# RWKV projections: the next tile's raw keys are loaded a step sooner, the key row goes to another buffer and ahead of the bonus product, and the table loads and removals are reordered

## The chip, the cores and the metric

One core of one Trainium2 chip. The metric is the device time of the whole program in microseconds. The kernel before was run three times: median 3709.45 us, from 3708.74 to 3713.39.

## The reference, cut to what is computed

The program is two blocks of layers over 1024 tokens of width 1024, in fp32. The change is in the RWKV layer of the second block, in the stage that makes its six streams. The part that matters:

```python
xx = token_shift(hn) - hn
xs = hn[None] + xx[None] * mu[:, None, None, :]
r, k, v, g = jnp.einsum('pbsd,pdf->pbsf', xs[:4], w_in)
w_log = -jax.nn.softplus(-(w0 + jnp.tanh(xw @ w1) @ w2)) - 0.5
decay = jnp.exp(-jnp.exp(w_log.astype(jnp.float32)))
a = jax.nn.sigmoid(a0 + (xa @ a1) @ a2)
kk = (k * k_k).reshape(B, S, H, N).astype(jnp.float32)
kk = kk / jnp.maximum(jnp.linalg.norm(kk, axis=-1, keepdims=True), 1e-12)
k = k * (1.0 + (a - 1.0) * k_a)
# the scan over time uses r, decay, k, v, kk, a; then
bonus = jnp.sum(rh * kh * r_k, axis=-1, keepdims=True) * vh
```

## The kernel before

`rwkv_projections` (L3879) runs from about 2559 to 3081 us of the span. Its main loop has sixteen steps j: four streams (k, r, v, g) of four steps, each step two tiles of 128 tokens. A step is a product of two tiles by a 1024x1024 weight, done in seven sums of eight matmuls instead of eight (`Seven`, L950): TensorE's order in a step is sum 5, sum 6, sum 3, sum 7, then sum 1 of the next step, sum 4, and sum 2 of the next step. GpSimd (POOL below) makes the operand sums s1, s2, s4, s3 for the step after; it runs about a step ahead. VectorE takes results out of PSUM (p15, u2, then the removals c12, c22, c21; L1040 to L1060) and ends each step with `mix(j + 2)`: a subtraction (L4137) and eight multiply-adds (L4140). ScalarE (ACT below) copies p1 and removes c11. Each engine works in the order in which its instructions are written; the semaphores only hold it up.

Beside steps 5, 6, 8, 9, 10, 12, 13 and 14 (`STEP_OF`, L3646) runs one tile of `ScanRows` (L3640), which turns the raw rows of the streams, read back from DRAM, into the rows that the scan of the next stage reads: cumulated decays, normed keys, the x, r, b and k rows, and the bonus. Its buffers are eight 128x1024 rows: `row_r`, `row_k`, `row_a`, `row_w`, `kk`, `t1`, `upto`, `back`. For one tile:

- SP loads `row_k`, `row_a`, `row_w`, `row_r` (L3697 to L3708), each once the rows in that buffer have been used or stored; the load of `row_a` waits until the b row of the tile before has landed in DRAM (L3707).
- POOL makes the keys `kk` (L3811); ACT squares them into `back` (L3782), makes `t1` = a - 1 (L3787), and the exponential `upto` of the decay sums (L3791) that TensorE makes from `row_w` (L3774). ACT then takes Ln of the head sums (L3793), the reciprocal decays into `back` (L3795), the norm (L3797), scales sixteen heads (L3801) and takes the exponential of `row_w` (L3803).
- VectorE reduces the squares (L3843, L3845), adds to the decay sums (L3850), and makes the key in `row_k` (L3861), the r row (L3868), the b scaling (L3855), the bonus rows (L3874) and their sums (L3876). In its order, the key and the r row stand between c12 and c22, the b scaling and the bonus between c22 and c21.
- POOL makes less (`t1` times k_a, L3816), the bonus product (L3821), the x row (L3827), the b row (L3832) and the k row (L3838); SP stores them.

In a POOL step the order is: keys, s1, less, s2, s4, bonus product, s3, x row, b row, k row. On SP the order in a step with a tile is: c11 store, ends, c12 store, c22 store, x row store with the next `row_w` load, c21 store, r row store with the next `row_r` load, b row store, k row store with the next loads of `row_k` and `row_a`. The activation tables are loaded by the compiler in front of each function that the present table lacks; `one_table` (L125) asks for a table that holds both Ln and Exp.

Of the kernel before, what the change touches and what calls it, by code (L numbers as in the profile page):

```python
# [10 lines left out]
ACT = mybir.ActivationFunctionType  # L11
# [3628 lines left out]
class ScanRows:  # L3640
# [95 lines left out]
    def sp_b_row(self, sp, i):  # L3736
        sp.wait_ge(self.q["b_row_made"], i + 1)
        sp.dma_start(self.raw[5][self.at(i), :], self.row_a).then_inc(self.q["b_stored"], 16)

    def sp_k_row(self, sp, i):  # L3740
        sp.wait_ge(self.q["k_row_made"], i + 1)
        sp.dma_start(self.raw[1][self.at(i), :], self.back).then_inc(self.q["k_stored"], 16)
        if i + 1 < X_TILES:
            self.sp_load_k(sp, i + 1)
            self.sp_load_a(sp, i + 1)

    def sp_rows(self, sp):
        first = self.at(0)
# [28 lines left out]
    def act_rows(self, act, i):  # L3777
        q = self.q
        act.wait_ge(q["kk_made"], i + 1)
        if i:  # L3780
            act.wait_ge(q["k_stored"], i * 16)
        act.activation(self.back, self.kk, ACT.Square).then_inc(q["squared"], 1)  # L3782
        act.wait_ge(q["ones_made"], 1)
        act.wait_ge(q["a_in"], (i + 1) * 16)
        if i:
            act.wait_ge(q["key_made"], i)
        act.activation(self.t1, self.row_a, ACT.Identity, bias=self.minus_one[:, :]).then_inc(q["less_made"], 1)  # L3787
        act.wait_ge(q["L_made"], i + 1)
        if i:
            act.wait_ge(q["r_stored"], i * 16)  # L3790
        act.activation(self.upto, self.sum_banks, ACT.Exp).then_inc(q["upto_decayed"], 1)  # L3791
        act.wait_ge(q["sums_floored"], i + 1)
        act.activation(self.norm[:, :], self.norm[:, :], ACT.Ln).then_inc(q["ln_made"], 1)  # L3793
        act.wait_ge(q["before_summed"], i + 1)
        act.activation(self.back, self.sum_banks, ACT.Exp, scale=-1.0).then_inc(q["back_decayed"], 1)  # L3795
        act.wait_ge(q["ln_made"], i + 1)
        act.activation(self.norm[:, :], self.norm[:, :], ACT.Exp, scale=-0.5).then_inc(q["rnorm_made"], 1)  # L3797
        act.wait_ge(q["rnorm_made"], i + 1)
        for h in range(W_HEADS):
            one = self.kk[:, h * W_DIM:(h + 1) * W_DIM]  # L3800
            last = act.activation(one, one, ACT.Copy, scale=self.norm[:, h:h + 1])  # L3801
        last.then_inc(q["kk_normed"], 1)
        act.activation(self.row_w, self.row_w, ACT.Exp).then_inc(q["own_decayed"], 1)  # L3803
# [30 lines left out]
    def pool_k_row(self, pool, i):  # L3834
        q = self.q
        pool.wait_ge(q["key_made"], i + 1)
        pool.wait_ge(q["b_row_made"], i + 1)
        pool.tensor_tensor(self.back, self.row_k, self.back, ALU.mult).then_inc(q["k_row_made"], 1)  # L3838

    def dve_sums(self, dve, i):  # L3840
        q = self.q
# [37 lines left out]
def rwkv_projections(nc, core, a, raw, weights, room, scan, row_sums):  # L3879
# [8 lines left out]
    with ExitStack() as mem:  # L3888
# [44 lines left out]
        with nc.Block() as block:  # L3933

            @block.sync
            def _(sp):
                sp.dma_start(norm_columns[:, :], columns_of(a["norm_gain_2"][1]), allow_slow_non_contiguous=True).then_inc(small_in, 16)
                for n in range(6):
                    sp.dma_start(mu[:, n, :], columns_of(a["odd_mu_2"][0, n]), allow_slow_non_contiguous=True).then_inc(mu_in, 16)
                for m, (down, up, bias) in enumerate((("rwkv_w1_2", "rwkv_w2_2", "rwkv_w0_2"), ("rwkv_a1_2", "rwkv_a2_2", "rwkv_a0_2"))):  # L3940
                    sp.dma_start(w_down[:, m, :, :], weight_blocks(a[down][0])).then_inc(lora_in, 16)
                    sp.dma_start(w_up[0:LO, m, :], a[up][0]).then_inc(lora_in, 16)
                    sp.dma_start(w_up[LO:LO + 1, m, :], a[bias][0].unsqueeze(0)).then_inc(lora_in, 16)
                scan.sp_constants(sp)

                def store(j, made, count, src, n, half, stored):
                    i = 2 * (j % PAIRS) + n
                    sp.wait_ge(made, count)
                    sp.dma_start(raw[stream(j)][i * P:(i + 1) * P, half * BANK:(half + 1) * BANK], src).then_inc(stored, 16)

                def store_low(i, m):
                    sp.wait_ge(low_moved, 2 * i + m + 1)
                    sp.dma_start(raw[(W, A)[m]][i * P:(i + 1) * P, :], low_rows[:, m, :]).then_inc(low_stored[m], 16)

                for j in range(J):
                    gated = stream(j) == G
                    q = j % PAIRS + 1
                    lows = [(i, m) for i in LOW_TILES.get(j, ()) for m in range(2)]
                    tile = scan.tile_at(j)
                    store(j, seven.c11_read, j + 1, s11, 0, 0, stored11)  # L3960
                    if tile is not None:
                        scan.sp_ends(sp, tile)
                    for i, m in lows[0:2]:
                        store_low(i, m)
                    store(j, *((silu12_made, q) if gated else (seven.c12_read, j + 1)), s12, 0, 1, stored12)
                    for i, m in lows[2:3]:
                        store_low(i, m)
                    if j % PAIRS == PAIRS - 1 and j + PAIRS + 1 < J:
                        sp.wait_ge(seven.made7, j + 1)
                        weights.load(sp, [f"{letter[stream(j + PAIRS + 1)]}{n}" for n in range(2)])  # L3970
                    if j == J - PAIRS - 1:
                        sp.wait_ge(seven.made7, j + 1)
                        sp.wait_ge(stored11, (2 * PAIRS + 1) * 16)
                        sp.wait_ge(stored12, (2 * PAIRS + 1) * 16)
                        scan.sp_rows(sp)
                    store(j, *((silu22_made, q) if gated else (seven.c22_read, j + 1)), s22, 1, 1, stored22)
                    for i, m in lows[3:5]:
                        store_low(i, m)
                    if tile is not None:
                        scan.sp_x_row(sp, tile)  # L3980
                    store(j, *((silu21_made, q) if gated else (seven.c21_read, j + 1)), s21, 1, 0, stored21)
                    for i, m in lows[5:6]:
                        store_low(i, m)
                    if tile is not None:
                        scan.sp_r_row(sp, tile, stored_by_tile)
                        scan.sp_b_row(sp, tile)
                        scan.sp_k_row(sp, tile)
                    if j == 2:
                        for m in range(2):
                            sp.wait_ge(low_stored[m], NT * 16)  # L3990
                        weights.load(sp, ("r0", "r1"))
                        sp.wait_ge(low_made, 2 * NT)
                        scan.sp_gains(sp)
                        scan.sp_spill(sp)
                    if j == PAIRS:
                        scan.sp_first(sp, stored_by_tile)
                scan.sp_all_stored(sp)
                for stored in (stored11, stored12, stored22, stored21):
                    sp.wait_ge(stored, J * 16)

            @block.gpsimd
            def _(pool):
# [6 lines left out]
                for j in range(J):  # L4009
                    pa, pb = pair_set(j)  # L4010
                    tile = scan.tile_at(j - 1)
                    if tile is not None:
                        scan.pool_keys(pool, tile)
                    pool.wait_ge(mix_made, j + 1)
                    seven.pool_s1(pool, j, pb)
                    if tile is not None:
                        scan.pool_less(pool, tile)
                    seven.pool_s2(pool, j, pa)
                    seven.pool_s4(pool, j, pa)
                    if tile is not None:  # L4020
                        scan.pool_bonus(pool, tile)
                    seven.pool_s3(pool, j, pa, pb)
                    if tile is not None:
                        scan.pool_x_row(pool, tile)
                        scan.pool_b_row(pool, tile)
                        scan.pool_k_row(pool, tile)

            @block.scalar
            def _(act):
# [49 lines left out]
                for j in range(J):  # L4079
                    gated, last = stream(j) == G, j == J - 1  # L4080
                    lows = LOW_TILES.get(j, ())
                    fronts = [i for i in (EARLY + 2 * j, EARLY + 2 * j + 1) if i < NT]
                    tile = scan.tile_at(j)
                    if tile is not None:
                        scan.act_rows(act, tile)
                    if lows:
# [1072 lines left out]
```

## Time and profile before

| what | us |
|---|---|
| median of three runs | 3709.45 |
| the profiled execution | 3713.88 |
| its span | 3712.1 |
| PE (matmul) busy | 3467.2 (93%) |
| VectorE busy | 1865.9 (50%) |
| ACT busy | 1154.8 (31%) |
| POOL busy | 864.9 (23%) |

The profile is of one execution; times in it are counted from the span's start. TensorE is busy for 93% of the span and the chain that ended last runs through it nearly throughout, so what counts is where it pauses. The granted clock is that of TensorE, in parts of its full 2.4 GHz. In a timeline, each row gives start, length, engine, line, operation, what it writes and reads, how many were merged, and in brackets how long the engine sat idle before it and what ended that.

### The profile page before, as it was taken

To read this page: it belongs to the slowest core of one execution; us is meant where nothing else is said; L and a number is where in the kernel's file an instruction comes from. 1 tells how busy PE (TensorE), PEld (TensorE's weight loads), DVE (VectorE), ACT (ScalarE), POOL (GpSimd) and SP (SyncE) were. 2 spreads that over 40 slices of the span, in tenths; PEclk is the share of its full clock that TensorE was granted. 3 is DMA by queue.
4 is the path that set the end of the run, shared out by engine and by line. 5 is a ranking of instruction groups with operands and counts; after the bars stand their busy time and mean duration, and the time that the engine had idled before them with its cause. 6 is when DMAs were issued, how large, how long until landed. Compare 5 with 4: busy or idle time off the path is not lost. (4 is left out here: it accounts for less than half of the span.)

```text
span 3712.1 us, 64726 instructions
## 1 busy us (share of the span) xinstructions
PE 3467.2 (93%) x27290; PEld 2028.3 (55%) x27290; DVE 1865.9 (50%) x2911; ACT 1154.8 (31%) x2214; POOL 864.9 (23%) x544
## 2 busy tenths in 40 slices
PE   8999999999998999899999999998899997887998
PEld 3447874445555777544455447444444335877543
DVE  3336652323218999631466228224658874665322
ACT  1127760102224555311311028112213352221124
POOL 0000003440000000242333210333126660333532
PEclk9999999999998999999999999999999998998999
DMA  6000013226235455510522020111264535443400
GB/s 244 29 23 2 2 45 127 88 71 173 77 102 143 126 134 133 196 46 17 181 81 80 0 91 2 68 46 18 89 235 174 201 135 155 118 113 82 165 12 40
DMA packets 312102, 358.43 MB, mean 97 GB/s; under 512 B 161540, under 2 KB 215028, under 8 KB 309126
## 3 DMA queue, kind: packets, MB, share of 16 engines
q1 hardware_dynamic: 311816, 354.30, 29.8%
q8 instruction: 218, 3.57, 0.4%
q14 instruction: 68, 0.56, 0.0%
HBM read 255.88 MB, written 98.29 MB: 95 GB/s over the span
## 5 line engine op out<-in xcount | busy, mean ns | idle before, releaser
L2200 DVE TENSOR_SCALAR_CACHE_REDUCE la_s<-psum 128x1280 f32<-128x1280 f32 x128 | 190.7, 1491 | 35.3 <-PE psum L2244 27.6
L2169 ACT ACTIVATE la_s<-la_s,la_negm 128x1280 f32<-128x1280 f32 x128 | 174.4, 1362 | 82.2 <-DVE la_s L2200 82.2
L970 POOL TENSOR_TENSOR lg_seven_s<-other_columns 128x512 f32<-128x512 f32 x4 | 5.1, 1264 | 732.3 <-POOLq L112 711.8
L991 PE MATMUL psum<-room,x_rows 128*128 128x512 f32 x320 | 145.6, 598 | 5.7 <-POOL x_rows L970 5.7
L970 POOL TENSOR_TENSOR wg_seven_s<-other_columns 128x512 f32<-128x512 f32 x5 | 6.3, 1268 | 592.3 <-POOLq L112 544.6
L835 DVE CUSTOM_DVE_ANT_0 wa_s<-psum,window_mask_rows 128x640 f32<-128x640 f32 (+1 forms) x128 | 100.6, 786 | 71.6 <-PE psum L890 71.6
L3328 POOL TENSOR_TENSOR x_rows<-x_rows,pg_g 128x512 f32<-128x512 f32 x56 | 84.0, 1500 | 153.7 <-DVE pg_g L3477 140.2
L991 PE MATMUL psum<-room,rp_seven_s 128*128 128x512 f32 x256 | 115.2, 593 | 3.2 <-DVE rp_seven_p L1040 3.2
L793 ACT ACTIVATE wa_s<-wa_s,wa_negm 128x640 f32<-128x640 f32 (+2 forms) x160 | 117.3, 742 | 0.4 <-DVE wa_negm L838 0.3
L991 PE MATMUL psum<-rp_t,rp_seven_s 128*128 128x512 f32 x256 | 117.0, 600 | 0.0
L991 PEld LDWEIGHTS psum<-room,x_rows 128*128 128x128 f32 x320 | 60.5, 192 | 77.8 <-issue 77.8
L786 ACT ACTIVATE wa_pT<-psum 128x512 f32<-128x512 f32 (+1 forms) x160 | 80.4, 552 | 64.0 <-PE psum L900 63.8
L890 PE MATMUL psum<-window_kT,window_qT 64*128 64x256 f32 (+1 forms) x800 | 95.6, 366 | 2.9 <-DVE wa_s L832 1.2
L2244 PE MATMUL psum<-first_weights,latent_qr 32*128 32x320 f32 x1024 | 94.3, 435 | 0.0
L927 PE MATMUL psum<-wa_pT,window_v 128*64 128x128 f32 x1344 | 91.5, 279 | 0.5 <-ACT wa_oT L808 0.2
L2208 DVE STREAM_TRANSPOSE la_pT<-la_s 128x1280 f32<-128x1280 f32 x64 | 90.1, 1474 | 0.0
L2208 DVE STREAM_TRANSPOSE x_rows<-la_s 128x1280 f32<-128x1280 f32 x64 | 90.1, 1473 | 0.0
L991 PE MATMUL psum<-rp_t,rp_mixed 128*128 128x512 f32 x128 | 70.0, 698 | 20.9 <-DVE x_rows L1056 20.9
L991 PE MATMUL psum<-pg_t,pg_seven_s 128*128 128x512 f32 x192 | 86.3, 592 | 0.0
L991 PEld LDWEIGHTS psum<-room,rp_seven_s 128*128 128x128 f32 x256 | 48.3, 190 | 64.2 <-issue 64.2
L900 PE MATMUL psum<-ident,wa_s 128*128 128x128 f32 x576 | 81.9, 283 | 0.3 <-ACT wa_s L793 0.3
L890 PEld LDWEIGHTS psum<-window_kT,window_qT 64*128 64x128 f32 x800 | 69.7, 187 | 22.4 <-issue 12.6
(719 smaller groups left out, 7947.4 us busy)
## 6 DMA issues: line engine op xcount, KB each, us to landing
x_rows<-rwkv_raw SPq DMA_DIRECT2D x40, 512.0 KB, 4.8
room<-rwkv_raw SPq DMA_DIRECT2D x33, 512.0 KB, 5.2
later_slot<-in_ada_w_dram SPq DMA_DIRECT2D x16, 1024.0 KB
rwkv_raw<-x_rows SPq DMA_DIRECT2D x64, 256.0 KB, 2.9
rwkv_raw<-x_rows SPq DMA_DIRECT2D x32, 512.0 KB, 4.2
room<-in_odd_w_in_dram SPq DMA_DIRECT2D x6, 2048.0 KB, 13.0
first_weights<-latent_v SPq DMA_DIRECT2D x32, 320.0 KB, 5.4
la_v<-latent_v SPq DMA_DIRECT2D x32, 320.0 KB, 5.5
```

What stands on the lines that cost most here:

```text
L786: act.activation(pT[:, u % 2, b, :, :].rearrange("p t q -> p (t q)")[:, 0:n], pT_banks[b][:, 0:n], ACT.Copy).then_inc(pT_moved, 1)
L793: act.activation(s_sb[:, u % 2, b, 0:n], s_sb[:, u % 2, b, 0:n], ACT.Exp, scale=SCALE, bias=negm[:, par, k:k + 1], accum_out=total[:, par, ...
L835: dve.tensor_tensor_reduce(out=s_sb[:, u % 2, b, 0:n], in0=s_banks[b][:, 0:n], in1=mask[:, lo:lo + n], scale=1.0, scalar=NEG, op0=ALU.add, ...
L890: last = pe.matmul(s_banks[b][:, at:at + n * P], qT[rows, p, t * P:(t + 1) * P], kT[rows, p // 4, k * P:(k + n) * P], start=True, stop=True)
L900: last = pe.transpose(pT_banks[b][:, n * P:(n + 1) * P], s_sb[:, u % 2, b, n * P:(n + 1) * P], core.ident)
L927: last = pe.matmul(o_bank[rows, (p % 4) * P:(p % 4 + 1) * P], v[:, k, g * A_DIM:(g + 1) * A_DIM], pT[:, u % 2, b, n, :], start=(n == 0), s ...
L991: last = pe.matmul(bank, left[:, k, :], right[:, k, :], start=fresh and k == 0, stop=k == HK - 1, skip_group_check=True)
L2169: act.activation(s, s, ACT.Exp, scale=-1.0, bias=negm[:, u % RING:u % RING + 1], accum_out=total[:, head(u) % 2, tile(u):tile(u) + 1]).the ...
L2200: dve.tensor_scalar(by_lane(s_sb[:, u % RING, :]), by_lane(banks_of(scores_side(u)))[:, :, 0:SPAN], -SCALE, FAR, ALU.mult, ALU.min, accum_ ...
L2208: dve.transpose(pT[h % 2][:, t, :], s_sb[:, u % RING, :]).then_inc(turned, 1)
L2244: last = pe.matmul(core.banks(scores_side(u) * LANE_GROUPS + r)[:, 0:SPAN], left, right, start=(b == 0), stop=(b == NOPE_BLOCKS))
L3328: pool.tensor_tensor(rows, rows, g[:, :], ALU.add).then_inc(x_made, 1)
```

## The change

- SP: the load of the next `row_a` moves from the k row's step to right behind the b row's store. The k row is stored from `t1` instead of `back`, and this store and the load of the next `row_k` move ahead of the x row's store; the load of `row_k` now waits for `bonus_rows` (L3874), since the b row's step no longer stands before it.
- POOL: the order becomes s1, less, s2, s4, k row (into `t1`), bonus product, x row, s3, b row, keys of the next tile. Only the keys of tile 0 stay at the head of a step.
- ACT: the exponential `upto` moves ahead of the `t1` row, which now waits for the k row's store (its buffer) instead of the square.
- ACT: `one_table` is asked for before tile 0 and before each tile of the gated steps (12 to 14), where Silu takes the table away.

```diff
@@ sp_b_row, sp_k_row
         sp.dma_start(self.raw[5][self.at(i), :], self.row_a).then_inc(self.q["b_stored"], 16)
+        if i + 1 < X_TILES:
+            self.sp_load_a(sp, i + 1)
...
-        sp.dma_start(self.raw[1][self.at(i), :], self.back).then_inc(self.q["k_stored"], 16)
+        sp.dma_start(self.raw[1][self.at(i), :], self.t1).then_inc(self.q["k_stored"], 16)
         if i + 1 < X_TILES:
+            sp.wait_ge(self.q["bonus_rows"], i + 1)
             self.sp_load_k(sp, i + 1)
-            self.sp_load_a(sp, i + 1)
@@ act_rows
         act.wait_ge(q["kk_made"], i + 1)
-        if i:
-            act.wait_ge(q["k_stored"], i * 16)
         act.activation(self.back, self.kk, ACT.Square).then_inc(q["squared"], 1)
-        act.wait_ge(q["ones_made"], 1)
-        act.wait_ge(q["a_in"], (i + 1) * 16)
-        if i:
-            act.wait_ge(q["key_made"], i)
-        act.activation(self.t1, self.row_a, ACT.Identity, bias=self.minus_one[:, :]).then_inc(q["less_made"], 1)
         act.wait_ge(q["L_made"], i + 1)
         if i:
             act.wait_ge(q["r_stored"], i * 16)
         act.activation(self.upto, self.sum_banks, ACT.Exp).then_inc(q["upto_decayed"], 1)
+        act.wait_ge(q["ones_made"], 1)
+        act.wait_ge(q["a_in"], (i + 1) * 16)
+        if i:
+            act.wait_ge(q["k_stored"], i * 16)
+        act.activation(self.t1, self.row_a, ACT.Identity, bias=self.minus_one[:, :]).then_inc(q["less_made"], 1)
@@ pool_k_row
         pool.wait_ge(q["key_made"], i + 1)
-        pool.wait_ge(q["b_row_made"], i + 1)
-        pool.tensor_tensor(self.back, self.row_k, self.back, ALU.mult).then_inc(q["k_row_made"], 1)
+        pool.wait_ge(q["back_decayed"], i + 1)
+        pool.tensor_tensor(self.t1, self.row_k, self.back, ALU.mult).then_inc(q["k_row_made"], 1)
@@ SP's steps
                     if tile is not None:
+                        scan.sp_k_row(sp, tile)
                         scan.sp_x_row(sp, tile)
...
                         scan.sp_b_row(sp, tile)
-                        scan.sp_k_row(sp, tile)
@@ POOL's steps
-                    if tile is not None:
+                    if tile == 0:
                         scan.pool_keys(pool, tile)
...
                     if tile is not None:
+                        scan.pool_k_row(pool, tile)
                         scan.pool_bonus(pool, tile)
+                        scan.pool_x_row(pool, tile)
                     seven.pool_s3(pool, j, pa, pb)
                     if tile is not None:
-                        scan.pool_x_row(pool, tile)
                         scan.pool_b_row(pool, tile)
-                        scan.pool_k_row(pool, tile)
+                        if tile + 1 < NT:
+                            scan.pool_keys(pool, tile + 1)
@@ ACT's steps
                     tile = scan.tile_at(j)
+                    if tile == 0 or tile is not None and gated:
+                        one_table(act)
                     if tile is not None:
                         scan.act_rows(act, tile)
```

## Rows read from the trace of the kernel before

**Rows 1.** Windows by step (6, 7, 11, 12, 14): length, busy times, clock, DMA share.
```profile
2795.39:2828.29 32.90, 28.15 (x61) 12.10 (x60) 25.41 (x23) 12.87 (x27) 22.74 (x11) 0.90 0.45 159
2828.29:2854.93 26.64, 24.54 (x57) 10.47 (x56) 23.15 (x19) 1.19 (x2) 14.29 (x7) 1.00 0.87 313
...
2943.61:2970.70 27.09, 24.54 (x58) 10.47 (x57) 23.60 (x19) 2.48 (x3) 14.74 (x7) 1.00 0.80 292
2970.70:2996.45 25.75, 25.75 (x62) 11.40 (x61) 21.25 (x23) 17.22 (x32) 16.00 (x8) 1.00 0.14 50
...
3028.84:3061.14 32.30, 27.98 (x62) 11.83 (x61) 21.91 (x21) 17.33 (x32) 21.79 (x11) 0.95 0.45 165
```
**Rows 2.** TensorE's waits, steps 5 to 15: total, times, longest.
```profile
PE psum L991 <- DVE x_rows L1056: 20.2, 8, 4.8
```
**Rows 3.** Timeline of PE: decay sums, fourth sum of 6, third of 7, fourth of 14.
```profile
2798.82 1.88 PE L3774 MATMUL psum<-x_rows,rs_decay_upto 128*128 128x512 f32 x4
...
2819.19 5.83 PE L991 MATMUL psum<-rp_t,rp_mixed 128*128 128x512 f32 x8 [4.75 <-DVE x_rows L1056]
...
2836.71 3.67 PE L991 MATMUL psum<-room,rp_seven_s 128*128 128x512 f32 x8 [1.39 <-DVE rp_seven_p L1040]
...
3051.34 5.40 PE L991 MATMUL psum<-rp_t,rp_mixed 128*128 128x512 f32 x8 [3.45 <-DVE x_rows L1056]
```
**Rows 4.** Timeline of SP's queue, tile 0 into tile 1.
```profile
2793.72 0.43 SPq L3700 DMA_DIRECT2D x_rows<-rwkv_raw  x1
...
2797.72 0.32 SPq L3738 DMA_DIRECT2D rwkv_raw<-x_rows  x1
...
2800.56 0.46 SPq L3703 DMA_DIRECT2D x_rows<-rwkv_raw  x1
2804.21 0.32 SPq L3708 DMA_DIRECT2D x_rows<-rwkv_raw  x1
```
**Rows 5.** Timeline of POOL: b row of tile 0, keys of tile 1.
```profile
2793.30 4.39 POOL L3832 TENSOR_TENSOR x_rows<-x_rows 128x1024 f32<-128x1024 f32 x1
...
2806.77 2.35 POOL L3811 TENSOR_TENSOR x_rows<-x_rows,rp_squares 128x1024 f32<-128x1024 f32 x1 [6.59 <-issue]
```
**Rows 6.** Transfers' landing: all row loads (page), then L3708 and L3738 alone.
```profile
x_rows<-rwkv_raw SPq DMA_DIRECT2D x40, 512.0 KB, 4.8
...
DMA to landing us min/median/max: 4.1/4.2/6.0
...
DMA to landing us min/median/max: 3.6/5.3/7.0
```
**Rows 7.** Timeline of ACT: the row t1 of tile 1.
```profile
2810.11 1.13 ACT L3787 ACTIVATE x_rows<-x_rows,rs_minus_one 128x1024 f32<-128x1024 f32 x1
```
**Rows 8.** Timeline of VectorE: mixes, keys, bonus rows and p15.
```profile
2769.40 3.26 DVE L4140 SCALAR_TENSOR_TENSOR rp_mixed<-rp_mixed,rp_mu,rp_hT 128x256 f32<-128x256 f32 x8
...
2782.58 1.67 DVE L3861 SCALAR_TENSOR_TENSOR x_rows<-x_rows 128x1024 f32<-128x1024 f32 x1
...
2792.89 2.60 DVE L4137 TENSOR_TENSOR rp_mixed<-rp_hT 128x2048 f32<-128x2048 f32 x1
...
2821.97 2.28 DVE L3874 TENSOR_TENSOR x_rows<-x_rows 128x1024 f32<-128x1024 f32 x1
...
2828.64 7.32 DVE L4140 SCALAR_TENSOR_TENSOR rp_mixed<-rp_mixed,rp_mu,rp_hT 128x256 f32<-128x256 f32 x8
2835.89 0.68 DVE L1040 TENSOR_TENSOR rp_seven_p<-psum,rp_seven_p 128x512 f32<-128x512 f32 x1
...
2867.82 1.73 DVE L3861 SCALAR_TENSOR_TENSOR x_rows<-x_rows 128x1024 f32<-128x1024 f32 x1
...
2951.65 0.67 DVE L1040 TENSOR_TENSOR rp_seven_p<-psum,rp_seven_p 128x512 f32<-128x512 f32 x1
```
**Rows 9.** Timeline of ACT in an earlier stage: preload, then Ln and Exp.
```profile
1728.00 1.28 ACT L127 ACT_TABLE_LOAD   x1
...
1730.80 0.20 ACT L190 ACTIVATE lg_next_stat<-lg_next_stat 128x1 f32<-128x1 f32 x1
```

## Prediction

> **What bounds the kernel now.** I read the windows by step first. A plain step of this stage costs TensorE 24.03 us (seven sums of 3.43), a step with a tile of scan rows 25.75 (1.72 more for the decay sums). The windows show steps 5, 8 and 12 at 25.75, the second and third tile of a run (6, 9, 10, 13, 14) at 30.7 to 32.9, and steps 7 and 11 at 26.6 and 27.1 [rows 1]. Over what the products alone need, that is 31.8 us in the five and 5.7 us in the two; with 0.9 in step 15 it is about 38 us, 1.0% of the span. Nothing outside this stage is touched, so 38 us is all there is to win.
>
> The waits of TensorE then name the gate: eight waits for L1056 (the c22 removal) hold 20.2 us of its idle time [rows 2]. The order of PE shows the price of one: in step 6 the fourth sum starts at 2819.19 instead of 2814.4, and runs 5.83 instead of 3.60 us, because the granted clock is down after the pause (0.90 in that window, 1.00 in its neighbours) [rows 1, 3]. Without three short ones of 0.7 to 0.8 us the five pauses are 17.9 us (3.0 to 4.8 each); the five slow sums after them (5.40 to 6.66, first and last shown) cost 11.8 us more [rows 3]. The pause of 1.39 us in step 7 has no slow sum behind it (3.67) [rows 3]. In step 7 the late one is L1040, p15, behind the mix.
>
> Who is late for L1056? It stands in VectorE's order behind the head sums (L3843), which read ACT's square; the square reads the keys (POOL 2806.77, made at 2809.1), and these the raw keys that SP asks for at 2800.56 [rows 4, 5]. So the keys are the gate that the change moves. But the row of a is right behind: SP asks for it at 2804.21, once the stored b row has landed, and it lands 4.2 us later, at 2808.4 [rows 4, 6]. ACT's L3787 uses it at 2810.11 [rows 7]. The slack is 1.7 us.
>
> **A second resource.** VectorE's eight mix steps take 3.26 us alone and 7.32 with POOL's rows beside them; POOL's b row product takes 4.39 where a row alone takes 2.35, VectorE's L3874 2.28 behind POOL's s3 [rows 5, 8]. The ends fit one waiting for the other: POOL's b row starts at 2793.30, VectorE's subtraction (from 2792.89, 2.60 long) ends at 2795.5, and the b row 2.2 later, at 2797.7. So POOL's products and VectorE's products of two SBUF operands go one at a time; after a wait a POOL row costs 2.2, and a VectorE row, by the same subtraction (L3874 ends 2824.25, s3 1.1 before it), 1.1. The Trainium skill (SBUF — State Buffer, Who interferes with whom) says the same: VectorE with two SBUF inputs and GpSimd share a port pair, held for a whole instruction. By that rule, the trace agrees, moving POOL work cannot make it overlap this VectorE work. It speaks against the change: the keys' 2.2 us now fall between the removals and the next p15.
>
> **Part by part.**
> - *Table loads.* L3793 and L3795 load one each for every tile, 1.28 us, and these go; in the gated steps L3791's becomes the preload; a preload (L127) with Ln and Exp behind it and no load between is in the stage at 1728 us [rows 9]. The new ones stand ahead of the wait for the keys, where ACT idles. All that follow the square now stand behind L3787, ahead of what VectorE needs last, so I count nothing; if the normed rows were late, up to 2 us a step would return.
> - *The exponential ahead of L3787.* 1.05 us later for tile 0, hidden: the key L3861 there ends at 2784.25 by waiting for c12 and POOL [rows 8]. The same holds in steps 8 and 12.
> - *POOL's order.* From that key end at 2784.25 in step 5 I line up what takes turns: r row 1.1, k row 2.2, b scaling 1.1, bonus product 2.2, x row 2.2, L3874 1.1, s3 1.15, b row 2.2: the b row is made at 2797.6, as now (2797.7). Then the mix's subtraction 2.15, keys 2.2, mix 3.26, p15 0.7: p15 at 2805.9. VectorE's reduction and c21 lie beside s3 and the b row. Now its sum begins without a wait at 2803.97 (decay sums 2798.82, 1.72 and 3.43 on) [rows 3]: a new pause of 1.9.
> - *SP, raw keys.* The load then waits for L3874 (2794.3) and lands 4.8 later, 2799.1, in time for the slot at 2799.8 [rows 6].
> - *SP, the w row.* It and the x row's store stand behind that wait and load: asked at 2795.2 instead of 2793.72 [rows 4]. At 4.8 to 5.8 (I take 5.3) it lands at 2800.5, and the decay sums, at 2798.82 before [rows 3], wait 1.7. In step 6 p15 hides it. In 10 and 14, where TensorE arrives sooner, the pause is near 4 us, with a slow clock (2.3).
> - *SP, the a row.* It moves past the k row's store, but its gate, the b row's landing, stays. That took 6.4 us here, 5.3 in the median, 7.0 at most [rows 4, 6]; a 512 KB load more now runs ahead of it, one k store less behind it. Bounds 5.3 and 7.2, I take 6.3. So a lands at 2797.7+6.3+4.2 = 2808.2, the same as before; L3787 ends at 2809.4 instead of 2811.2.
> - *From there.* POOL less 2.3, s2 1.15, key 1.1 (ends 2814.0), s4 1.15, r row 1.1, c22 0.65: 2816.9 instead of 2819.1. TensorE wants it at 2814.3+1.9 = 2816.2, so 0.7 of pause and no slow sum. Step 7 starts at 2823.8 instead of 2828.3.
> - *And back.* p15 of step 7 is the key's end 2814.0 + s4 1.15 + 21.65 (the list above) = 2836.8, where it was 2836.6 [rows 8]. TensorE is there at 2830.7. It waits 6 us instead of 1.4, and the pauses of 3 us and more cost 1.8 to 3.1 of slow clock each, which that of 1.4 did not [rows 3]. So what step 6 gave is returned in step 7.
>
> **Sum.** Steps 5 to 7: +0.2, and 0 to 2.5 of slow clock. A round from key to key is 14.5 to the b row, 6.3+4.2 of transfers, 1.25 L3787, 2.3, 1.15, 1.1, and 0.1: 30.9. Steps 8 to 11: key end 2869.5 (as now), +13.4+16.4 = 2899.3, +30.9 = 2930.2, p15 of step 11 22.8 on at 2953.0 against 2952.3 [rows 8]: +0.7, and 0 to 2.5. Step 12 starts 115.8 after step 8 [rows 1], so steps 12 to 15: keys end at 2985.3, 3015.05 and 3045.95, c22 of step 14 at 3048.9 (its sum waits till 3051.34 now [rows 3]); no mix follows tile 7, so nothing takes it back. TensorE reaches the fourth sum of 14 at 3050.2 (w row lands 3032.4, decay 1.7, slow clock 2.3, four sums) and step 15 at 3057.0 instead of 3061.14 [rows 1]: -4.1. With half of the two slow clocks (+2.5): 0.2+0.7+2.5-4.1 = -0.7. The profiled execution took 3713.88 (span 3712.1), so it would be 3713.2; against the median 3709.45, 3708.7. Bounds: the b landing at 5.3 gives five rounds back 1 us each (-5.7), at 7.2 takes 0.9 each (+3.8); slow clocks give ±2.5.
>
> **Rivals.**
> - *The keys were the only gate.* The c22 pauses and their slow sums go: 17.9+11.8 = 29.7, 3680. For it: all five pauses hang on rows behind the keys. Against: a's slack of 1.7 and the port's queue ending at 2836.8. 10%.
> - *The turns are kinder.* Keys slip behind p15 (raw keys landing after the mix) or the port's queue has gaps: 2.2 less a round in steps 7 and 11, no slow clock there (2.5 less), the last run gains 2.5 more by an unslowed step 14, and its two rounds are 1 us shorter: 4.4+2.5+2.5+2 = 11.4, 3697.3. Against: a landing of over 8 us is in no row. 15%.
> - *Slower: the w row starves the decay sums.* If it lands 6.3 rather than 5.3 after its issue behind the raw keys, TensorE's p3 and with it c12 and the next key are set by it: x row made + 2.1 + 6.3 + 1.7+3.4+2.3+3.4+0.8, a round of 31.1 or more with a slow clock in each. The gain of step 14 goes (+4), both slow clocks count whole (+2.5), and five rounds lose 0.5 each: +9, 3717.7. It decides from a landing of 6.0. 15%.
> - *It does not do what it says*: the table preloads are there and unused, or the load of raw keys lands as late as now. Time as now, 5%.
>
> **How the numbers follow.** The forecast has 55%, and with it the last rival falls within 0.2% (7.4 us, about what a measurement tells from no change); I give 2 of the 55 to faster. Faster 0.10+0.15+0.02 = 0.27, same 0.58, slower 0.15. The range goes from 3697 (the kinder turns) to 3719 (the w row), and leaves out the first rival and about a third of each edge.
>
> **What would show it.** Right: keys of tile 1 end near 2802, the square waits little; L3787 starts by a's landing near 2808.3; c22's pauses shrink below 1 us; new pauses at L3774 and at p15 in steps 6, 7, 10, 11; one preload before tile 0 and none in tiles 1 to 4. Wrong: a landing before 2806, p15 of step 7 before 2834, or slow sums gone in all steps.

## The result

The changed kernel takes 3721.38 us (median of 16 runs) where the kernel before takes 3710.54 (16 runs): a ratio of 1.0027, with a 95% interval of 1.0019 to 1.0035. It is slower by about 10 us, small but clear of its interval. The forecast was 3708.7 us and "the same", with a range from 3697 to 3719.

The two profiled executions differ by 17.4 us in their spans (3712.1 and 3729.5), more than the medians do: the changed kernel's is the slowest of its 16 (3731.30). Of the 17.4, step 5 starts 3.7 us later already, in code that is the same, and 2.3 us lie behind step 15, where the code is the same too. What the change does lies between the start of step 5 and that of step 15. I call this the stretch and read it from TensorE's timeline: 291.5 us before, 302.9 after. It splits into three parts, one for each run of tiles:

| part | before | after | difference | forecast |
|---|---|---|---|---|
| steps 5 to 7 | 85.3 | 90.1 | +4.8 | +0.2, and half of 2.5 |
| steps 8 to 11 | 115.8 | 122.5 | +6.7 | +0.7, and half of 2.5 |
| steps 12 to 14 | 90.4 | 90.3 | -0.1 | -4.1 |
| sum | 291.5 | 302.9 | +11.4 | -0.7 |

The windows of steps 6, 7, 11, 12 and 14 of the kernel after answer to [rows 1] (length, busy times of PE, its weight loads, VectorE, ACT and POOL, granted clock, DMA share, GB/s):

```profile
2799.06:2829.76 30.70, 27.95 (x61) 11.81 (x60) 24.34 (x22) 10.53 (x25) 20.47 (x10) 0.94 0.48 172
2829.76:2863.42 33.66, 26.97 (x57) 11.41 (x56) 26.15 (x22) 1.19 (x2) 12.11 (x8) 0.90 0.70 244
...
2952.57:2985.93 33.36, 27.34 (x58) 11.57 (x57) 25.48 (x22) 2.48 (x3) 11.69 (x7) 0.90 0.63 228
2985.93:3011.68 25.75, 25.75 (x62) 11.40 (x61) 19.41 (x21) 14.13 (x29) 17.18 (x8) 1.00 0.16 53
3041.74:3076.22 34.48, 28.96 (x61) 12.28 (x60) 27.32 (x23) 14.76 (x30) 23.31 (x12) 0.90 0.43 156
```

Step 6 is 2.2 us shorter than before, as it should be; steps 7 and 11, which have no tile of their own, are 7.0 and 6.3 us longer, and step 14 is 2.2 longer. TensorE's waits of the kernel after, from step 5 on, answer to [rows 2] (who, for whom, total, times, longest):

```profile
PE psum L3776 <- issue: 16.6, 5, 5.1
PE psum L991 <- DVE rp_seven_p L1040: 11.3, 2, 6.0
PE psum L991 <- DVE x_rows L1056: 2.3, 3, 0.8
```

The five long waits for c22, 17.9 us in all, are gone, as planned. In their place stand five waits at the decay sums (L3774 before, L3776 now) and two for p15. The timeline of PE shows three of them, and the slow sums behind:

```profile
2805.30 2.38 PE L3776 MATMUL psum<-x_rows,rs_decay_upto 128*128 128x512 f32 x4 [2.64 <-issue]
2807.47 4.91 PE L991 MATMUL psum<-rp_t,rp_seven_s 128*128 128x512 f32 x8
...
2842.77 6.10 PE L991 MATMUL psum<-room,rp_seven_s 128*128 128x512 f32 x8 [5.98 <-DVE rp_seven_p L1040]
...
2964.90 6.47 PE L991 MATMUL psum<-room,rp_seven_s 128*128 128x512 f32 x8 [5.30 <-DVE rp_seven_p L1040]
```

"issue" at the decay sums means that the profile shows no engine that released them. What they need last is the w row, a transfer. SP's queue in tile 0, to be held against [rows 4]:

```profile
2798.14 0.32 SPq L3703 DMA_DIRECT2D x_rows<-rwkv_raw  x1
2798.50 0.43 SPq L3725 DMA_DIRECT2D rwkv_raw<-x_rows  x1
2798.97 0.43 SPq L3700 DMA_DIRECT2D x_rows<-rwkv_raw  x1
2799.99 0.76 SPq L3949 DMA_DIRECT2D rwkv_raw<-x_rows  x1
2800.79 0.81 SPq L3731 DMA_DIRECT2D rwkv_raw<-x_rows  x1
2801.72 0.52 SPq L3697 DMA_DIRECT2D x_rows<-rwkv_raw  x1
2802.28 0.45 SPq L3738 DMA_DIRECT2D rwkv_raw<-x_rows  x1
2809.65 0.32 SPq L3708 DMA_DIRECT2D x_rows<-rwkv_raw  x1
```

Seven transfers go out within 4.6 us: raw keys, x row, w row, c21, r row, next r row, b row. The last of these has landed 7.4 us after its issue, at 2809.65, when SP asks for the a row. The landings of the kernel after, for L3738 (b row), L3700 (w row) and L3725 (x row):

```profile
DMA to landing us min/median/max: 3.8/7.5/8.2
...
DMA to landing us min/median/max: 3.9/6.1/6.6
...
DMA to landing us min/median/max: 2.6/5.3/5.6
```

For the b row that is 7.5 where it was 5.3 [rows 6]. The w row took 4.7 in the median before, and the x row 2.9. Who waits for these landings is in the timelines of ACT and POOL (tile 1):

```profile
2804.16 2.34 POOL L3811 TENSOR_TENSOR x_rows<-x_rows,rp_squares 128x1024 f32<-128x1024 f32 x1 [2.61 <-DMA rwkv_raw<-x_rows]
```
```profile
2814.02 1.15 ACT L3791 ACTIVATE x_rows<-x_rows,rs_minus_one 128x1024 f32<-128x1024 f32 x1 [5.29 <-DMA x_rows<-rwkv_raw]
```

The keys of tile 1 start 5.1 us into step 6 (2804.16 less 2799.06), where they started 11.4 us into it before [rows 5], and even so they have waited for the stored x row. The row t1 then waits 5.3 us for the a row, and starts later than before: 14.96 us after the start of step 6, where it was 14.72 [rows 7].

### The profile page after: what moved, and what is told of

Same layout as the page of the kernel before. It is cut to its first block and busy times, and to the rows that moved or that the text cites. A ratio compares the mean times of both kernels' runs of the same rounds, so it can differ in the third digit from the quotient of the medians.

```text
span 3729.5 us, 64703 instructions
## 1 busy us (share of the span) xinstructions
PE 3478.7 (93%) x27290; PEld 2033.3 (55%) x27290; DVE 1871.6 (50%) x2911; ACT 1134.8 (30%) x2198; POOL 860.0 (23%) x544
## 5 line engine op out<-in xcount | busy, mean ns | idle before, releaser
L2208 DVE STREAM_TRANSPOSE la_pT<-la_s 128x1280 f32<-128x1280 f32 x64 | 90.1, 1474 | 0.0
L2208 DVE STREAM_TRANSPOSE x_rows<-la_s 128x1280 f32<-128x1280 f32 x64 | 90.1, 1474 | 0.0
L991 PEld LDWEIGHTS psum<-rp_t,rp_seven_s 128*128 128x128 f32 x256 | 51.3, 202 | 65.5 <-issue 65.4
## 6 DMA issues: line engine op xcount, KB each, us to landing
room<-in_odd_w_in_dram SPq DMA_DIRECT2D x6, 2048.0 KB, 12.8
```

Source lines behind the costliest of these rows:

```text
L991: last = pe.matmul(bank, left[:, k, :], right[:, k, :], start=fresh and k == 0, stop=k == HK - 1, skip_group_check=True)
L2208: dve.transpose(pT[h % 2][:, t, :], s_sb[:, u % RING, :]).then_inc(turned, 1)
```

## The experiments

All but one column of this table come from one profiled execution of each kernel; landings are medians from issue to landing of the four row transfers, in us. The ratio is of the whole kernel to the one before, on the same chip, with its 95% interval. The stretch is the finer measure: it leaves out what varies in the 2770 us ahead of it and the 650 behind. There is one trace of each kernel, so how far the stretch varies from one execution to the next isn't measured; differences of 1 or 2 us I don't build on.

| kernel | w row | raw keys | b row | a row | stretch | ratio |
|---|---|---|---|---|---|---|
| before | 4.7 | 4.9 | 5.3 | 4.2 | 291.5 | 1 |
| changed | 6.1 | 4.3 | 7.5 | 4.1 | 302.9 | 1.0027 (1.0019 to 1.0035) |
| a gate off | 6.1 | 4.5 | 7.6 | 4.4 | 291.7 | 0.9999 (0.9988 to 1.0010) |
| keys behind w | 4.7 | 5.3 | 6.6 | 4.1 | 296.2 | 1.0006 (0.9995 to 1.0018) |
| keys behind p15 | 6.0 | 4.5 | 7.3 | 4.1 | 295.6 | 1.0015 (1.0004 to 1.0026) |
| before, a gate off | 4.7 | 5.2 | 5.3 | 6.1 | 292.4 | 1.0008 (0.9997 to 1.0019) |
| r store early | 6.0 | 4.2 | 6.7 | 4.1 | 298.0 | 1.0015 (1.0005 to 1.0025) |
| no preloads | 6.0 | 4.5 | 7.4 | 4.1 | 303.8 | 1.0032 (1.0021 to 1.0043) |
| before, one store more | 5.7 | 6.9 | 7.3 | 4.1 | 301.0 | 1.0013 (1.0003 to 1.0022) |
| reordered | 4.2 | 4.6 | 3.0 | 4.8 | 282.6 | 0.9976 (0.9964 to 0.9989) |
| before, r store early | 4.7 | 5.2 | 4.0 | 5.4 | 293.2 | 0.9999 (0.9986 to 1.0013) |
| before, preloads | 4.7 | 4.9 | 5.2 | 4.6 | 290.1 | 0.9992 (0.9979 to 1.0005) |
| reordered, t1 first | 4.1 | 4.6 | 2.9 | 4.9 | 280.2 | 0.9977 (0.9965 to 0.9988) |
| same, keys sooner | 4.1 | 4.9 | 5.1 | 4.1 | 283.1 | 0.9988 (0.9975 to 1.0001) |

Two theories stood against each other. The landing theory: the load of the raw keys has been put ahead of the x, w, r and b transfers, each of them lands later for it, and the a row, gated by the b row, most. The port theory: POOL's and VectorE's products go one at a time, and the keys now take a turn between the removals and p15. The k row's store, which the change moves too, is not in the burst: in tile 0 it leaves SP at 2791.45, 6.7 us ahead of the raw keys' load, and it lands in 2.9 us in the median.

**The a gate off.** The a rows in two buffers, so that no stored b row holds the next load up. The second buffer is that of r_k, and the bonus product takes the row of k_k in its place, so this kernel's bonus is another number at the same cost (cut to the load):

```diff
@@ sp_load_a
-        if i:
-            sp.wait_ge(self.q["b_stored"], i * 16)
-        sp.dma_start(self.row_a, self.raw[5][self.at(i), :]).then_inc(self.q["a_in"], 16)
+        if i > 1:
+            sp.wait_ge(self.q["b_stored"], (i - 1) * 16)
...
+        sp.dma_start(self.a_of(i), self.raw[5][self.at(i), :]).then_inc(self.q["a_in"], 16)
@@ sp_b_row
-        if i + 1 < X_TILES:
-            self.sp_load_a(sp, i + 1)
@@ sp_k_row
         if i + 1 < X_TILES:
+            self.sp_load_a(sp, i + 1)
             sp.wait_ge(self.q["bonus_rows"], i + 1)
```

> The changed kernel, with the raw a rows in two buffers by turns, so that the next one is loaded with the k row's store and waits for no stored b row (the second buffer is the one of r_k; the bonus product uses k_k's row instead, so the bonus is another number at the same cost). Steps 5 to 15 took 291.5 us before the change and 302.9 after. Landing theory (the loss comes from transfers that queue behind the raw keys' load, the a row first): L3791 starts without a wait for a transfer, rounds from key to key fall from 33.0-33.5 to about 30, and the stretch takes 294 to 297 us; the pauses at the decay sums stay, since the w row stays where it is. Port theory (the loss is the keys' turn between the removals and p15): p15 comes 22.7 us after the key's end all the same and the stretch stays above 300 us.

The stretch fell by 11.2 us, to 291.7, which is nearly all that the change had cost (11.4); 294 to 297 was expected. The ratio says the same: 0.9999, its interval clear of the changed kernel's. The row t1 of tile 1 now follows the square and the exponential without a wait (timeline of ACT; the first row is the square, the last t1):

```profile
2804.01 1.06 ACT L3787 ACTIVATE x_rows<-x_rows 128x1024 f32<-128x1024 f32 x1 [6.14 <-POOL x_rows L3816]
2804.97 1.01 ACT L3791 ACTIVATE x_rows<-psum 128x1024 f32<-128x1024 f32 x1
2805.88 1.14 ACT L3796 ACTIVATE x_rows<-rp_r_k,rs_minus_one 128x1024 f32<-128x1024 f32 x1
```

The b row lands as late as in the changed kernel (7.6), but nobody waits for it. The pauses at the decay sums stay (2.2 to 3.9 us), as do two for p15 (3.9 and 3.8 us). So the wait for the a row is the largest cost, and the port theory alone is not enough: it had wanted more than 300.

**The raw keys behind the w row.** Same kernel as the changed one, but for SP's order:

```diff
@@ sp_k_row
-            sp.wait_ge(self.q["bonus_rows"], i + 1)
-            self.sp_load_k(sp, i + 1)
@@ sp_x_row
             self.sp_load_w(sp, i + 1)
+            sp.wait_ge(self.q["bonus_rows"], i + 1)
+            self.sp_load_k(sp, i + 1)
```

> The changed kernel, with the load of the raw keys (and its wait for the bonus rows) moved behind the x row's store and the load of the w row. Landing theory: the w row is asked for 1.6 us sooner and with one transfer less ahead of it, so it lands about 2.5 us sooner and the pauses at the decay sums (2.6, 2.3, 4.4, 2.2, 5.1 us) shrink by about that much; the a row lands as late as now, so c22 and p15 don't move and the stretch of 302.9 us falls by 0 to 3. Port theory: no change within 1 us.

The w row lands in 4.7 us again, and four of the five pauses at the decay sums are gone; the fifth is 2.2 us (TensorE's waits of that kernel):

```profile
PE psum L991 <- DVE rp_seven_p L1040: 21.1, 7, 5.9
PE psum L991 <- DVE x_rows L1056: 6.6, 7, 2.2
PE psum L3775 <- issue: 2.2, 1, 2.2
```

The gain of 6.7 us is more than the 0 to 3 expected. The b row lands in 6.6 instead of 7.5, which I had not counted on; the pauses for p15, now seven, show that it stays the next one late. The direction is the landing theory's, the size was not mine.

One thing more stands in the two timelines of PE. All of TensorE's pauses in the stretch sum to 29.8 us in the changed kernel and to 29.1 here: as much idle time, in more pieces. What fell is TensorE's busy time for the same matmuls, from 273.0 to 267.1 us, at a granted clock of 0.97 in the stretch instead of 0.94. So most of the 6.7 us came back through the clock: five of the seven pauses for p15 are only 1.8 to 2.1 us long, and four of these have no slow sum behind them. The edit takes away two things at once, the load ahead of the x and w rows and SP's wait for `bonus_rows` ahead of them (in the changed kernel the x row is made at 2797.02 and stored at 2798.50); the runs don't part them.

**The keys behind p15.** One wait more for POOL:

```diff
                         if tile + 1 < NT:
+                            pool.wait_ge(seven.p15_read, j + 1)
                             scan.pool_keys(pool, tile + 1)
```

> The changed kernel, with one wait more: POOL makes the next keys only once VectorE has made p15 of the step. Port theory: p15 follows 20.5 instead of 22.7 us after the key's end, the pauses at p15 in steps 7 and 11 (6.0 and 5.3 us) shrink by 2.2 each, the keys come about 3 us later but still before the a row lands, and the stretch falls from 302.9 to about 298. Landing theory: p15 is held up in the same measure by what comes before, the stretch stays within 1.5 us of 302.9.

The mix before p15 of step 6 (VectorE's timeline, first of this kernel, then of the changed one):

```profile
2801.55 3.26 DVE L4145 SCALAR_TENSOR_TENSOR rp_mixed<-rp_mixed,rp_mu,rp_hT 128x256 f32<-128x256 f32 x8
```
```profile
2803.74 5.43 DVE L4144 SCALAR_TENSOR_TENSOR rp_mixed<-rp_mixed,rp_mu,rp_hT 128x256 f32<-128x256 f32 x8
```

The mix is free of POOL and 2.2 us shorter, and the pauses for p15 in steps 7 and 11 fall by 2.1 and 1.8 us (to 3.9 and 3.5). The landings are as in the changed kernel. A wait was added and the stretch fell by 7.3 us, more than the 5 expected; the ratio, 1.0015, is not clear of the changed kernel's. So by the traces the port theory is right too, for the two steps that have no tile; 4 us of the 7.3 are these pauses, 1.9 more the shorter slow sums behind them (5.33 and 5.37 instead of 6.10 and 6.47).

**Before, with the a gate off.** The same two buffers in the kernel before, its queues else as they were, with the same other bonus.

> The kernel before, with the raw a rows in two buffers by turns, at the same places in the queues (k_k's row in the bonus product, as in the run with the a gate off). If the a row has 1.7 us of slack in the kernel before, as the forecast read it, the stretch of 291.5 us stays within 1 us; if the a row is a gate there too, it falls by 3 us or more.

No gain: 292.4 against 291.5. The a row was no gate in the kernel before, as the forecast read from [rows 4, 6, 7].

**The r row's store early**, ahead of the k row's store:

```diff
                     if tile is not None:
+                        scan.sp_r_row(sp, tile)
                         scan.sp_k_row(sp, tile)
                         scan.sp_x_row(sp, tile)
...
-                        scan.sp_r_row(sp, tile, stored_by_tile)
+                        scan.sp_next_r(sp, tile, stored_by_tile)
                         scan.sp_b_row(sp, tile)
```

> The changed kernel, with the r row's store moved ahead of the k row's store, where the r row has long been made; its load of the next r row stays. One 512 KB transfer less stands ahead of the b row's store. Landing theory: the b row lands some 1.2 us sooner than now (median 7.5 us from its issue in the changed kernel, 5.3 in the one before), the a row with it, and the stretch from step 5 to 15 falls from 302.9 to 298-300 us. If the landing is set by something else than the transfers ahead of it, nothing moves (within 1 us).

The b row lands in 6.7 instead of 7.5 us, and the stretch is 4.9 us shorter. One transfer less ahead is worth 0.8 us here, less than the 1.2 expected.

**No preloads**, the changed kernel without its two lines with `one_table`.

> The changed kernel without the asked-for table loads, so that Ln and Exp load their tables again. The forecast gave them nothing: in the changed kernel the normed rows are ready 2 to 3 us before VectorE and POOL use them, so 2.6 us more on ACT should cost 0 to 4 us in the stretch of 302.9. A rival (ACT has become the late one) would show 8 us or more.

303.8 against 302.9, within the 0 to 4 expected: the removed table loads are worth about nothing there, as counted.

**Before, one store more.** A second store of the x row, behind the first (POOL's keys of the next tile wait for it too, long after it has landed):

```diff
         sp.dma_start(self.raw[4][self.at(i), :], self.kk).then_inc(self.q["x_stored"], 16)
+        sp.dma_start(self.spare[self.at(i), :], self.kk).then_inc(self.q["extra_stored"], 16)
```

> The kernel before with one transfer more: the x row is stored a second time, into a DRAM tensor that nobody reads, right behind its store. Landing theory: each transfer of 512 KB queued ahead costs those behind it about 1.2 us, so the b row lands 6.5 instead of 5.3 us after its issue and the w row 5.9 instead of 4.7; the w row then comes about 1 us late for the decay sums, the a row uses 1.2 of its 1.7 us of slack, and the stretch grows from 291.5 by 1 to 4 us. If landings don't depend on what is queued, no change.

All that stand behind it land later: w 5.7 (4.7), b 7.3 (5.3), raw keys 6.9 (4.9). The stretch grows by 9.5 us, far more than the 1 to 4 that I expected. I had counted the a row's slack and forgotten the raw keys: they are behind the b row in this kernel's queue, they are its gate. From one key to the next it takes 0.4 us more in the first of the five rounds and 1.8 to 2.7 more in the other four, 9.5 in all. POOL's timeline has it for tile 3 (the kernel before, then this one; the key of tile 2 ends at 2869.55 and 2870.22):

```profile
2890.64 2.35 POOL L3811 TENSOR_TENSOR x_rows<-x_rows,rp_squares 128x1024 f32<-128x1024 f32 x1 [5.15 <-issue]
...
2894.02 2.35 POOL L3815 TENSOR_TENSOR x_rows<-x_rows,rp_squares 128x1024 f32<-128x1024 f32 x1 [7.88 <-DMA x_rows<-rwkv_raw]
```

So a single idle store, which nobody reads or waits for soon, costs nearly as much in the stretch as the change did (9.5 against 11.4 us). The whole kernel shows less of it: 1.0013, with an interval of 1.0003 to 1.0022, is 1 to 8 us.

**Reordered.** The changed kernel with SP's queue in the order in which the rows are due:

```diff
@@ sp_b_row
     sp.dma_start(self.raw[5][self.at(i), :], self.row_a).then_inc(self.q["b_stored"], 16)
     if i + 1 < X_TILES:
+        sp.wait_ge(self.q["bonus_rows"], i + 1)
+        self.sp_load_k(sp, i + 1)
+        self.sp_next_r(sp, i, r_stored)
         self.sp_load_a(sp, i + 1)
```

with the r row's store early, as above, and the raw keys' load taken out of the k row's step.

> The changed kernel with SP's order by due time: r row's store, k row's store, x row's store and w row load, c21 store, b row's store, then the loads of the raw keys and of r, and the a row last. Landing theory: w and b land as in the kernel before (4.7 and 5 us), the raw keys come when p15 is nearly made, so the keys hardly stand in its way; a round from key to key is 30 to 30.5 us, the pauses at p15 in steps 7 and 11 are 3 to 4 us, none above 2 at the decay sums or c22 but in steps 10 and 14; the stretch takes 285 to 290 us, less than the 291.5 of the kernel before, and the whole 0.05 to 0.2% less than before. Port theory alone: about as the run with the keys behind p15, 295.6.

The b row lands in 3.0 us, the w row in 4.2, and the stretch is 282.6 us, 20.3 less than the changed kernel and 8.9 less than the one before, better than the 285 to 290 expected, which had b and w landing in 5 and 4.7. Here too most of the gain on the kernel before is in the clock: TensorE's pauses sum to 20.9 us (23.5 before), its busy time is 261.7 (268.0 before), at a granted clock of 0.98 (0.95). The raw keys are asked for later than in the changed kernel, and come when the mix is over (POOL's and VectorE's timelines, tile 3; the second row is the mix, the third p15):

```profile
2888.35 2.54 POOL L3813 TENSOR_TENSOR x_rows<-x_rows,rp_squares 128x1024 f32<-128x1024 f32 x1 [5.12 <-DMA x_rows<-rwkv_raw]
```
```profile
2885.42 3.25 DVE L4146 SCALAR_TENSOR_TENSOR rp_mixed<-rp_mixed,rp_mu,rp_hT 128x256 f32<-128x256 f32 x8
2888.59 0.68 DVE L1040 TENSOR_TENSOR rp_seven_p<-psum,rp_seven_p 128x512 f32<-128x512 f32 x1
```

**Before, with the r row's store early**: that one move of SP's in the kernel before.

> The kernel before with one thing changed: the r row is stored ahead of the x row instead of behind c21, so one 512 KB transfer less stands ahead of the b row's store and of the raw keys' load. Landing theory: the b row lands about 1 us sooner than 5.3, the raw keys 0 to 1 us sooner than 4.9, and since the keys gate each round there, the stretch falls from 291.5 to 287-291 us. If landings don't depend on what is queued: no change.

A miss. The b row lands 1.3 us sooner (4.0), but the raw keys do not (5.2), since they are asked for when the k row is made, whatever the queue has done by then. The a row takes 5.4 instead of 4.2: it now goes out 1.5 us behind the keys' load in tile 0, 3.7 behind it before (with the a gate off it goes out 0.5 behind it, and takes 6.1). The two together take 9.4 us, 9.5 before. Taking a transfer out did not help here, since the gate, the raw keys, was asked for when the burst was over.

**Before, with the preloads** alone.

> The kernel before with the asked-for table loads alone. Counted at nothing by the forecast in the changed kernel. In the kernel before, Ln and the exponentials stand between the keys and the b scaling but behind the row t1: c22, which TensorE waits for, doesn't need them, so the stretch of 291.5 falls by 0 to 2 us; a rival, that ACT's 2.6 to 3.9 us a tile are on the path, would give 5 us or more.

290.1 against 291.5, within the 0 to 2 expected; the ratio can't tell it from no change.

**Reordered, t1 first.** As the reordered kernel, with ACT's order square, t1, exponential as in the kernel before.

> The reordered kernel (stretch 282.6) with ACT's row t1 back ahead of the exponential of the decay sums. There the a row lands 0.9 us before the square ends, so t1 no longer waits for it, and each round from key to key is shorter by the exponential's 1.0 us until the a row's own landing limits it (0.9): the stretch falls by 3 to 5 us, to 278-280, and the whole to 0.9960-0.9975 of the kernel before.

280.2 us, 2.4 less than the reordered kernel, a little short of the 3 to 5; the ratio, 0.9977, is just outside the 0.9960 to 0.9975 expected. The waits for c22 fall from 1.6 to 1.0 us each, while ACT's p1 becomes late in the gated steps (TensorE's waits of this kernel):

```profile
PE psum L991 <- DVE rp_seven_p L1040: 8.6, 3, 3.9
PE psum L991 <- DVE x_rows L1056: 7.4, 8, 1.0
...
PE psum L991 <- ACT rp_seven_p L1033: 2.0, 2, 1.0
```

That ratio doesn't set it apart from the reordered one (0.9976).

**The same, keys sooner.** The load of the raw keys ahead of the b row's store.

> As the run before, but with the raw keys' load ahead of the b row's store instead of behind it: asked about 1.5 us sooner. Both theories agree on the sign: the b row and with it the a row land about 1 us later and become the gate, and the keys take their turn at the port before p15 again (mix 5.3 instead of 3.3 us). The stretch grows by 3 to 8 us against the run before. If sooner keys were worth having, it would fall.

283.1 us, 2.9 more than the run before, just under the 3 to 8 expected; the ratios' intervals overlap (0.9988 and 0.9977). The b row lands 2.2 us later (5.1), and the mix takes 5.34 us again. It is the pair of runs in which the raw keys' load alone changes place, past the b row's store: asking for the keys sooner makes the b row late and the mix long, and in the stretch it costs time.

## Why the prediction was wrong

**What held.** The a row was no gate before (the a gate off in the kernel before gave nothing); the size of its slack, 1.7 us, no run tests. The line-up of POOL's and VectorE's turns was right to a few tenths: the b row made 28.2 us after the start of step 5 (forecast 28.0), p15 of step 7 at 22.7 us after the key's end (22.8), 14.5 us from key to b row in the round from step 9 to 10 (14.5). The w row was asked for 25.7 us after the start of step 5 (25.6). New pauses came at the decay sums and at p15 of steps 7 and 11, and the c22 pauses shrank; in steps 6 and 10 none came for p15, where the forecast had one too, since the decay sums had held TensorE up already. The keys of tile 1 ended at 2806.5, 7.4 us into step 6, where the forecast had its step 6 at 6.6: they waited for the stored x row to land, which the sum had left out, and it cost nothing, as the a row came later still. The table loads were worth nothing.

**The steps that failed** are terms of the sum that were too small, two of them landings of transfers and the third the slow clock behind them:

- *The b row's landing*, "Bounds 5.3 and 7.2, I take 6.3". It measured 7.5, with 8.2 at most, outside the bounds; and in tile 0 the store itself left SP 0.7 us after the row was made, since the issues of the r rows ahead of it took 0.8 and 0.5 us. From the b row made to the a row asked for it is 8.1 us in tile 0 and 7.6 in tile 3, against 6.3 in the sum. Taking the wait for it away gives back 11.2 us, more than any other single move in the changed kernel. I had added one place in the queue, at some 1 us, to the median of the old queue. The run with one store more in the kernel before shows the same: one place costs 2.0 us there.
- *The w row's landing*, "At 4.8 to 5.8 (I take 5.3)". It measured 6.1. In steps 6 and 9 the pause at the decay sums then is 2.3 to 2.6 instead of 1.7, with slow sums (in step 6 the decay sums take 2.38 for 1.88 and the sum behind them 4.91 for 3.60), where I had put none. In steps 10 and 14 it is 4.4 and 5.1 for "near 4 us". The late sum 3 makes c12 late, and so the key: in the round from 9 to 10 the key ends 33.5 us after the last one, 30.9 in the forecast; half of the 2.6 is the b row, the other half this.
- *The slow clock in steps 7 and 11*, "With half of the two slow clocks (+2.5)". Both came, in full: 6.10 and 6.47 for 3.60, 5.4 us for the 2.5 that was in the sum.

Together: steps 5 to 7 have 2.4 us from the later p15 and 2.5 from the slow sum, 4.8 in all. Steps 8 to 11 have 3.9 and 2.9. In steps 12 to 14 nothing is left of -4.1: the w row of step 14 is asked for 1.9 us later than forecast, the rounds before it being longer, and lands 0.9 later still, so the decay sums start 64.5 us after the start of step 12 instead of 61.7; the rest is the slow clock there (2.8 for 2.3) and a pause of 0.45 for p1.

Seen from TensorE, 6.3 of the 11.4 us are longer pauses (29.8 for 23.5) and 5.0 are busy time at a lower clock (273.0 for 268.0).

**The rivals.** The nearest was the slower one, "the w row starves the decay sums", at 15%, deciding from a landing of 6.0, with a time of 3717.7, 8.2 above the median before. The landing is 6.1, the loss 10.8, and part of it is what that rival described; it left out the a row. But taking the w row's lateness away gives back 6.7 of the 11.4 us, taking the a row's away 11.2, and moving the keys out of p15's way 7.3. These don't add up, since one late thing hides another. What they share is one transfer: the raw keys' load ahead of the others. With it behind the b row, and the r row's store early, all else of the change in place, the kernel is 0.24% faster than the one before (the r row's store early alone gives the changed kernel 4.9 us of the 20.3). A run with the load behind the b row and the r row's store where it was is not among these. How the 11.4 us split between the a row and the w row in the changed kernel stays open; the two meet at the key and no run took away just one without touching the other's queue, but for the a row.

The fault of method: I priced the landings of the changed queue from medians of the old one. [rows 4, 6] and the order of SP's steps were enough to see that the transfers would leave close together; what each place costs was not in them, and the bound should have reached two places further.

## What to carry to other kernels

A load that is moved ahead makes each transfer behind it in the same queue land later, here by 0.8 to 2.3 us for 512 KB (least the b row behind the r row's store, most the x row's store behind the keys' load, 5.3 for 3.0), and the ones to price are those on which the next round waits, not the one that is moved. Order a burst by when each row is due, the gate of the next round first; a load that comes sooner than its user can run is a cost, and where its user takes turns with an engine that TensorE waits for, it is one twice. When a wait is taken out of one step, look at what follows in the steps without such work: there the same round is late, and a longer pause brings slow sums with it. Idle time in several pauses below 2 us cost less than the same in one long one.

## What the runs showed of the hardware

A place in the queue has no fixed price. The b row's store of 512 KB lands in 2.9 us with little ahead of it, 4.0, 5.3 and 6.7 with more, and 7.5 at the end of the burst of seven; the w row's load goes from 4.1 to 6.1 (medians). SP's own issue takes longer too in such a burst: 0.32 us with nothing just ahead, 0.81 for the r row above, and up to 1.41 for the b row in the run with the keys behind the w row.

Whether TensorE's sums run slow behind a pause can be told from its length at the ends only. In the stretches of all fourteen traces, the 22 pauses of 1.3 to 1.9 us have no slow sum behind them, and all of 3.0 us and more have, at 1.5 to 3.1 us each. Of the 19 between, 12 have one and 7 have none, one of 2.88 us among them. In one kernel (the keys behind the w row) two pauses of the same length stand with different sums behind them:

```profile
2916.81 1.96 PE L3775 MATMUL psum<-x_rows,rs_decay_upto 128*128 128x512 f32 x4 [2.18 <-issue]
...
3025.15 5.40 PE L991 MATMUL psum<-rp_t,rp_mixed 128*128 128x512 f32 x8 [2.19 <-DVE x_rows L1056]
```

The second comes 12.7 us after another pause of 1.8, the first 12.8 us after one of 0.75; why the one is slow and the other isn't is not settled by these runs. For a forecast, a pause of 2 to 3 us should be priced with the slow clock and without.
